# Half feed-forwards' up phases: two of the four weight sums of each tile pair made by accumulating loads from GpSimd instead of by VectorE

## The reference, cut to what matters

```python
def swiglu(h, wg, wu, wd):
    return (jax.nn.silu(h @ wg) * (h @ wu)) @ wd

def half_ffn(h, g, shift, scale, gate, wg, wu, wd):
    return h + 0.5 * gate * swiglu(modulate(rms_norm(h, g), shift, scale), wg, wu, wd)

for l in range(DEPTH):                      # DEPTH = 2, d = 1024
    x   = half_ffn(x,   ..., ffn_w_gate[l, 0], ffn_w_up[l, 0], ffn_w_down[l, 0])
    ctx = half_ffn(ctx, ..., the same weights)
    ...                                     # token mixing
    x   = half_ffn(x,   ..., ffn_w_gate[l, 1], ffn_w_up[l, 1], ffn_w_down[l, 1])
    if l < DEPTH - 1:
        ctx = half_ffn(ctx, ..., the same weights)
```

## Time and profile before

| | |
|---|---|
| median of three runs | 2948.27 us |
| span of the profiled execution, the only time the profile gives for it | 2949.2 us |
| PE busy | 2864.6 us, 97% |
| DVE busy | 1701.3 us, 58% |
| ACT busy | 602.0 us, 20% |
| POOL busy | 37.6 us, 1% |
| DMA, SP's queue, ACT's queue, the software queue | 31.6%, 7.6%, 0.9% of the 16 engines |

### The profile page before, as it was taken

How to read it: one execution, slowest core, us unless ns; L and a number is a source line. 1 busy time by engine, 2 the same in 40 slices (tenths; PEclk the granted TensorE clock), 3 DMA queues, 4 the chain that set the end, 5 groups by cost and what they waited for, 6 DMA issues and landing times.

```text
span 2949.2 us, 41107 instructions
## 1 busy us (share of the span) xinstructions
PE 2864.6 (97%) x16754; PEld 2354.5 (80%) x16754; DVE 1701.3 (58%) x3407; ACT 602.0 (20%) x1371; POOL 37.6 (1%) x60
## 2 busy tenths in 40 slices
PE   8988999999999999999999999999999999999999
PEld 7777788977889888888644468888888888766999
DVE  3376467345566477773225457775377773235775
ACT  1254221134221210000124420100021000134110
POOL 0000000020000000000000000000000000000000
PEclk9999999999999999999999999999999999999999
DMA  6400465663665534423213034442444433322454
GB/s 239 139 2 3 147 235 151 193 167 109 221 209 151 190 136 164 149 87 90 91 39 114 1 129 157 158 123 64 129 156 157 148 88 80 116 80 86 144 145 113
DMA packets 349215, 376.15 MB, mean 128 GB/s; under 512 B 7299, under 2 KB 302612, under 8 KB 348260
## 3 DMA queue, kind: packets, MB, share of 16 engines
q1 hardware_dynamic: 323748, 285.68, 31.6%
q10 hardware_dynamic: 23072, 82.52, 7.6%
q0 software_dynamic: 2208, 5.31, 0.9%
HBM read 372.44 MB, written 1.05 MB: 127 GB/s over the span
## 4 chain that ended last, share of the span: by engine, by line
PE 92%; DVE 4%; ACT 3%; issue 1%; DMA 0%; SPq 0%; DVEq 0%; ACTq 0%
PE acc L134 76%; PE aux L134 14%; ACT sb_xn L302 1%; PE aux L2563 1%; DVE sb_work L1570 1%; DVE sb_big L1400 0%; DMA sb_work<-c_decay 0%; DVE sb_work L1400 0%; PE aux L2020 0%; ACT sb_rstd L290 0%; DMA sb_x<-xT 0%; DVE sb_xn L278 0%; ACT sb_rstd L292 0%; DVE sb_work L2792 0%; ACT sb_big L1087 0%
## 5 line engine op out<-in xcount | busy, mean ns | idle before, releaser
L134 PE MATMUL acc<-sb_xn,weights 128*128 128x256 f32 (+3 forms) x5184 | 1221.8, 389 | 17.8 <-DVE sb_xn L278 8.2
L134 PEld LDWEIGHTS acc<-sb_xn,weights 128*128 128x128 f32 (+1 forms) x5184 | 943.2, 190 | 248.2 <-issue 124.3
L134 PE MATMUL acc<-sb_work 128*128 128x256 f32 (+1 forms) x1944 | 374.1, 346 | 2.9 <-DVE sb_work L1575 2.9
L134 PEld LDWEIGHTS acc<-sb_work 128*128 128x128 f32 x1944 | 323.6, 191 | 38.2 <-issue 4.0
L134 PE MATMUL acc<-sb_work,weights 128*128 128x256 f32 (+2 forms) x1508 | 322.0, 361 | 5.8 <-DVE sb_work L1617 3.6
L134 PE MATMUL acc<-sb_big,weights 128*128 128x256 f32 (+1 forms) x1776 | 315.0, 334 | 4.2 <-issue 4.0
L134 PEld LDWEIGHTS acc<-sb_big,weights 128*128 128x128 f32 x1776 | 279.0, 192 | 31.1 <-issue 5.5
L134 PEld LDWEIGHTS acc<-sb_work,weights 128*128 128x128 f32 x1508 | 254.1, 191 | 53.5 <-issue 25.6
L1537 ACT COPY sb_work<-acc 128x256 f32<-128x256 f32 (+1 forms) x108 | 36.7, 340 | 684.0 <-PE acc L134 684.0
L1610 DVE TENSOR_TENSOR sb_work<-sb_work,acc 128x256 f32<-128x256 f32 (+1 forms) x112 | 42.6, 380 | 218.0 <-PE acc L134 218.0
L1543 ACT ACTIVATE sb_work<-sb_work 128x256 f32<-128x256 f32 (+1 forms) x88 | 34.4, 391 | 562.3 <-DVE sb_work L1624 562.3
(11 more groups left out here) (352 smaller groups left out, 2671.4 us busy)
## 6 DMA issues: line engine op xcount, KB each, us to landing
weights<-ffn_w_up SPq DMA_DIRECT2D x88, 1024.0 KB, 9.1
weights<-ffn_w_down SPq DMA_DIRECT2D x48, 1408.0 KB, 7.2
sb_work<-w_mod_rows ACTq DMA_DIRECT2D x100, 512.0 KB, 6.2
weights<-ffn_w_gate SPq DMA_DIRECT2D x44, 1024.0 KB, 5.5
sb_big<-w_mod_rows ACTq DMA_DIRECT2D x44, 512.0 KB, 4.8
weights<-mix_w_in SPq DMA_DIRECT2D x5, 2048.0 KB, 11.7
weights<-ple_w_gate SPq DMA_DIRECT2D x4, 2048.0 KB, 7.9
weights<-na_w_qkv SPq DMA_DIRECT2D x8, 1024.0 KB, 8.0
```

What stands on the lines that cost most here:

```text
L134: return te.matmul(o, lhsT, rhs, start=start, stop=stop, skip_group_check=True)
```

## The change

In tiles 2 to 21 of the up phase of each half feed-forward (`by_dma`), s1 and s3 are no longer made by DVE. POOL makes them with loads, for a pair of tiles at a time (`gpsimd_fast`), with three DMAs of 128 partitions by 4 by 256 numbers (512 KB) each:

- a plain load of the upper k-tiles of the up weights into a buffer (`sum_pairs`, two of them, in turn);
- an accumulating load of the lower k-tiles of the gate weights onto those of the up weights in the weight slot, which makes s3 there;
- once the first has landed, an accumulating load of the lower k-tiles of the up weights onto the buffer, which makes s1 of both tiles.

A load can add but not subtract here, so s3 becomes a11 + a21, and the signs of the other sums, of the copy of product 1 (now an ACTIVATE with scale -1) and of one read of product 3 are changed to suit. For pair b, POOL starts when product 6 of tile 2b-3 is done (the last reader of that buffer); for the first pair, when the input of the half feed-forward is complete. DVE's s2 and PE's product 5 now wait for the pair's sum, PE's product 7 for the sum in the slot. The two buffers need room: the rows keep two tiles where they had three. s2 and s4 stay on DVE, as do all four sums of tiles 0 and 1 and of the down phases. Semaphores used earlier in the program are used again for the new waits, so `masks_or_pair_sum_arrived` and `rwkv_up_or_pair_sum_arrived` are the two buffers' and `rpb_or_slot_sum_arrived0` to `3` the four slots'.

```diff
+    sum_up = [area(work, 3072 + 512 * n, 4, 128) for n in range(2)]
+    sum_pairs = [area(work, 4096 + 1024 * n, 4, 256) for n in range(2)]
-    row_cond, row_tile = area(work, 8192, 2, D), [area(work, at, D) for at in (10240, 11264, 4608)]
+    row_cond, row_tile = area(work, 8192, 2, D), [area(work, at, D) for at in (10240, 11264)]
...
+        def by_dma(self, i):
+
+            return 2 <= i < FT
...
             for q in FIRST_PRODUCTS if i == 0 else PRODUCTS:
-                if q in SUM_FOR:
-                    te.wait_ge(st_s.sem, F.s(4 * j + (SUMS if i else FIRST_SUMS)[SUM_FOR[q]]))
+                if q == 5 and F.by_dma(i):
+                    te.wait_ge(pair_sum[i // 2 % 2].sem, F.pair[i // 2])
+                elif q == 7 and F.by_dma(i):
+                    te.wait_ge(slot_sum[F.up[i // 2].slot].sem, F.slot[i // 2])
+                elif q in SUM_FOR:
+                    te.wait_ge(st_s.sem, F.s(i, SUM_FOR[q]))
...
-                st_u.on(ac.copy(u[:, s, :], bank_a[:, 0:F.H]))
+                st_u.on(ac.activation(u[:, s, :], bank_a[:, 0:F.H], ACT.Copy, scale=-1.0))
...
+    def gpsimd_fast(F, w_gate, w_up, x_ready):
+        gv, uv = (w.rearrange("(k p) n -> p k n", p=128) for w in (w_gate, w_up))
+        gp.wait_ge(x_ready[0].sem, x_ready[1])
+        for b in range(1, FH):
+            c, blk = slice(256 * b, 256 * b + 256), F.up[b]
+            if b >= 2:
+                gp.wait_ge(F.done[2 * b - 3, 6][0].sem, F.done[2 * b - 3, 6][1])
+            pair_sum[b % 2].on(gp.dma_start(sum_pairs[b % 2], uv[:, 4:8, c]))
+            gp.wait_ge(weights_in[blk.slot].sem, blk.arrived_at)
+            up_low = slots[blk.slot][:, 2048:3072].rearrange("p (k n) -> p k n", k=4)
+            slot_sum[blk.slot].on(gp.dma_start(up_low, gv[:, 0:4, c], accum_op=ALU.add))
+            gp.wait_ge(pair_sum[b % 2].sem, F.pair[b] - 16)
+            pair_sum[b % 2].on(gp.dma_start(sum_pairs[b % 2], uv[:, 0:4, c], accum_op=ALU.add))
...
         for n in which:
-            if n == 0:
-                for blk in F.blocks_of(i):
+            if n in (0, 2) and F.by_dma(i):
+                continue
+            if n == 0 or n == 1 and F.by_dma(i):
+                for blk in F.blocks_of(i - i % 2 if i < FT else i):
                     ve.wait_ge(weights_in[blk.slot].sem, blk.arrived_at)
+            if n == 1 and F.by_dma(i):
+                ve.wait_ge(pair_sum[i // 2 % 2].sem, F.pair[i // 2])
...
-            st_c12.on(ve.tensor_tensor(g2, g2, bank_e[:, 0:F.H], ALU.add))
+            st_c12.on(ve.tensor_tensor(g2, bank_e[:, 0:F.H], g2, ALU.subtract))
...
-        for M in (mix0, mix1):
-            gpsimd_heads(M.heads)
+        for F, M in ((half00, mix0), (half01, None), (half10, mix1), (half11, None)):
+            w = [ins[name][F.l, F.j] for name in ("ffn_w_gate_2", "ffn_w_up_2")]
+            gpsimd_fast(F.fast, *w, F.norm.x_ready[KT - 1])
+            if M is not None:
+                gpsimd_heads(M.heads)
```

More of the change, by code:

```diff
@@ L138, in build @@
     hy_in, x_in = signal("hyena_tables_arrived", 16), signal("x_arrived", 16)
-    ctx_in, up_in = signal("dft_and_context_arrived", 16), signal("rwkv_up_arrived", 16)
-    msk_in, rpb_in = signal("masks_arrived", 16), [signal(f"rpb_arrived{q}", 16) for q in range(4)]
+    ctx_in, up_in = signal("dft_and_context_arrived", 16), signal("rwkv_up_or_pair_sum_arrived", 16)
+    msk_in, rpb_in = signal("masks_or_pair_sum_arrived", 16), [signal(f"rpb_or_slot_sum_arrived{q}", 16) for q in range(4)]
     p_in = signal("p_arrived", 16)
@@ L1349, in build @@
     FH = FT // 2
-    sum_up = [area(work, 3072 + 512 * n, 4, 128) for n in range(3)]
+    sum_up = [area(work, 3072 + 512 * n, 4, 128) for n in range(2)]
+    sum_pairs = [area(work, 4096 + 1024 * n, 4, 256) for n in range(2)]
+    pair_sum, slot_sum = [msk_in, up_in], rpb_in
+    for sig, loads in ((msk_in, 2), (up_in, 3), *zip(rpb_in, (9, 8, 8, 8))):
+        sig.reserve(loads)
     sum_down = [area(work, 8192 + FH * 128 * n, FH, 128) for n in range(3)]
@@ L1430, in __init__ @@
             m = n - self.start
-            self.s, self.t = st_s.reserve(4 * m), st_t.reserve(8 if up else 4)
+            made = [4 * min(i, 2) + 2 * max(0, min(i, FT) - 2) + 4 * max(0, i - FT) if up else 4 * (i - FT) for i in range(n)]
+            count = st_s.reserve((2 * 4 + 2 * (FT - 2) if up else 0) + 4 * KT // 2)
+            self.s = lambda i, k: count(made[i] + ({1: 0, 3: 1}[k] if self.by_dma(i) else (SUMS if i else FIRST_SUMS)[k]))
+            self.t = st_t.reserve(8 if up else 4)
+            self.pair = {b: pair_sum[b % 2].reserve(2)(1) for b in range(1, FH)} if up else {}
+            self.slot = {b: slot_sum[self.up[b].slot].reserve(1)(0) for b in range(1, FH)} if up else {}
             self.u, self.b, self.v, self.d, self.c12, self.c21 = (s.reserve(m) for s in (st_u, st_b, st_v, st_d, st_c12, st_c21))
@@ L1454, in activations, with sums @@
             return [src[:, kt * h:kt * h + kt, self.H * t:self.H * t + self.H] for h in range(2) for t in range(2)]
+        def sums(self, i):
+            c = 128 * (i % 2)
+            return [sum_pairs[i // 2 % 2][:, :, c:c + 128]] + sum_up if i < FT else sum_down
         def blocks_of(self, i):
@@ L1474, in tensor_fast @@
             a11, a12, s3, a22 = F.weights(i)
-            s1, s2, s4 = sum_up if up else sum_down
+            s1, s2, s4 = F.sums(i)
             t1, t2, t4 = F.sum_x if up else F.sum_h
@@ L1522, in scalar_first_copy @@
         ac.wait_ge(F.done[0, 1][0].sem, F.done[0, 1][1])
-        st_u.on(ac.copy(F.temps[0][:, 0, :], bank_a[:, 0:F.H]))
+        st_u.on(ac.activation(F.temps[0][:, 0, :], bank_a[:, 0:F.H], ACT.Copy, scale=-1.0))
     def scalar_fast(F, following=None):
@@ L1553, in scalar_fast @@
             scalar_square(following, KT - 1)
+    def gpsimd_fast(F, w_gate, w_up, x_ready):
[11 more added lines that the diff above has]
+            pair_sum[b % 2].on(gp.dma_start(sum_pairs[b % 2], uv[:, 0:4, c], accum_op=ALU.add))
     def vector_weight_sums(F, i, which):
         a11, a12, a21, a22 = F.weights(i)
-        s1, s2, s4 = sum_up if i < FT else sum_down
+        s1, s2, s4 = F.sums(i)
         for n in which:
-            if n == 0:
-                for blk in F.blocks_of(i):
+            if n in (0, 2) and F.by_dma(i):
+                continue
+            if n == 0 or n == 1 and F.by_dma(i):
+                for blk in F.blocks_of(i - i % 2 if i < FT else i):
                     ve.wait_ge(weights_in[blk.slot].sem, blk.arrived_at)
+            if n == 1 and F.by_dma(i):
+                ve.wait_ge(pair_sum[i // 2 % 2].sem, F.pair[i // 2])
             if i not in (F.start, FT) and n != 2:
@@ L1565, in vector_weight_sums @@
                 ve.wait_ge(F.done[i - 1, q][0].sem, F.done[i - 1, q][1])
-            if n:
-                ve.wait_ge(st_s.sem, F.s(4 * (i - F.start) + (SUMS if i else FIRST_SUMS)[n] - 1))
-            to, one, other, op = ((s1, a21, a22, ALU.add), (s2, s1, a11, ALU.subtract),
-                                  (a21, a11, a21, ALU.subtract), (s4, a12, s2, ALU.subtract))[n]
-            st_s.on(ve.tensor_tensor(to, one, other, op))
+            if n and not (n == 1 and F.by_dma(i)):
+                ve.wait_ge(st_s.sem, F.s(i, {1: 0, 2: 1, 3: 1 if F.by_dma(i) or not i else 2}[n] if i or n != 2 else 3))
+            to, one, other = ((s1, a21, a22), (s2, s1, a11), (a21, a11, a21), (s4, a12, s2))[n]
+            st_s.on(ve.tensor_tensor(to, one, other, ALU.add))
     def vector_activation_sums(F, i):
@@ L1579, in vector_activation_sums @@
             vector_weight_sums(F, 0, (2,))
-        st_t.on(ve.tensor_tensor(b12, b22, b12, ALU.subtract))
+        st_t.on(ve.tensor_tensor(b12, b12, b22, ALU.subtract))
         ve.wait_ge(st_t.sem, st_t.n)
```

## The result

The changed kernel is slower by 0.8%: 2972.06 us in the median of four runs (2967.63 to 2976.64) against 2948.22 for the kernel before, a ratio of 1.008 [1.0067, 1.0092], which is 20 to 27 us. The profiled execution has a span of 2972.0 us, 22.8 more than that of before (2949.2). From here on a ratio in brackets is a 95% interval against the kernel before, and "up phase of `half11`" is the stretch from PE's wait at its start (2742.74 before) to its last wait (2876.30 before), 133.56 us.

A forecast was written before the change was run, and what follows sets the result against it. PE was taken to bound the kernel. The span 2949.2 + 10 (late loads in `half11`) - 0.5 (removed sums) = 2958.7 us, less 0.9 to the median 2957.8, stated as 2957; range 2947 to 3035.

The forecast's parts named there:

- What bounds the kernel: Whole kernel: PE makes 92% of the chain of waits, DVE 4%, so the removed work is hardly on the path.
- Removed, -0.5 us: DVE's 160 sums, 109 us, go; only waits at phase ends can shrink: 0.5 us, all in `half11`, bounds 0 and 6.2.
- Signs and ACT's copy, 0: DVE's adds keep their shape and ACT's copy becomes a same-shape ACTIVATE, covered by two products: zero.
- Wide phases, the sums hidden, 0: Wide phases: the last load lands at 19.4 us, due at about 28 after POOL may start, so zero cost.
- `half11`, +10 us: Up phase of `half11`: the third load lands late, holding DVE's s2 and then PE's product 4: 10 us over nine pairs.
- Every second pair is late: In `half11` a 2.3 us wait delays the next burst, so the next pair makes it: 1.15 us on the mean.
- hidden everywhere: Rival: the software queue gets turns beside SP's burst, so all loads are in time: 2948 us, chance 0.34.
- The price of the accumulation: DMA engines: an accumulating load takes k = 2.5 times a plain load's 1.42 us, so 3.55 us.
- The rows, 0: Two row buffers: a row is issued behind product 1 of its tile, DVE waits up to 1.7 us, hidden: zero.
- The cover of 5.2 us: Behind DVE's row wait stands the read of product 4, which PE needs three products, 5.2 us, later.
- The rival of late rows: Two row buffers: POOL's 1.5 MB a pair delay rows beyond the cover, so PE waits: 2954 to 2970 us, chance 0.05.
- what would show it: Signs: for, `half11` 5 to 25 us longer with product 4 waits; against, PE waits in wide phases or at product 7.

The follow-up runs named there:

- e9: The changed kernel with four pair buffers instead of two in `half11`, so POOL may start a pair's loads two pairs earlier: 2956.12 us, ratio 1.0024.
- e7: The changed kernel with no accumulating load and three row buffers, leaving the signs, ACT's scaled copy and product 3's turned read: 2947.49 us, ratio 0.9997.
- e5: The changed kernel with both passes of a row always in one tile: 2962.74 us, ratio 1.0047.
- e12: The changed kernel with accumulating loads only in the wide phases and both passes of a row in one tile: 2947.98 us, ratio 0.9996.
- e3: The changed kernel with accumulating loads only in `half11`, three row buffers and DVE's sums in the wide phases: 2961.2 us, ratio 1.0048.
- e4: The changed kernel with both accumulating loads as plain loads of the same size, so the sums are wrong: 2956.75 us, ratio 1.0035.
- e1: The kernel before with only the row buffers changed, two instead of three: 2967.63 us, ratio 1.007.
- e11: The kernel before with two row buffers and both passes of a row always in one tile: 2946.94 us, ratio 1.0.
- e10: The changed kernel with only the accumulation onto the weight slot made a plain load, so s3 is wrong: 2965.68 us, ratio 1.0055.
- e8: The kernel before with the rows ended at tile 18 instead of 20 and s4 of tile 22 made later: 2940.41 us, ratio 0.9972.
- e2: The changed kernel with accumulating loads only in the three wide phases, DVE making the sums in `half11`: 2958.04 us, ratio 1.003.

## Why the prediction was right, and where it was not

*What bounds the kernel: right.* PE is dense, of the removed 109 us of DVE less than 1 us came back as time, and whatever comes late in front of product 4 is paid in full and with a restart.

*Removed, -0.5 us: right.* In `half11` the 0.40 went and the 0.99 stayed (e9's 132.99 us against 133.56). The 0.35 us at the end of `half10` weren't foreseen.

*Signs and ACT's copy, 0: right* (e7).

*Wide phases, the sums hidden, 0: right* (e5, e12).

*`half11`, +10 us: the place and the chain right, 13.0 to 14.2 measured; that the size is so near is in part luck.* The wait is at product 4, released by the read of product 7, behind s2's wait for the third load, L1591 beyond 10 us, as forecast. The waits alone are 8.9 us (8.7 in e3, 9.9 in e5) for the forecast's 10. What the sum put at nothing is the restart, 0.54 us for each of seven waits, 3.8 in all, and the clock, 1.4.

The waits come out near 10 though their pattern is another one. "Every second pair is late" by 2.3 us is what the prediction has; in the changed kernel seven of nine pairs wait (eight in e3), 1.3 us each on the mean, and the first of them, the pair that the prediction works out, 1.67. The 2.3 us that a wait gives to the next pair were taken as pure gain; but SP's block hangs on the same product 4 and comes as much later, and the third load, which goes out 5 to 6 us after POOL's start, lands behind that block and not ahead of it. After the first wait SP's block is issued 5.2 us after POOL's start, where the working has 3.6. Waits of 1.67 and 0.55 follow each other, so some of the relief is there. The error of the same kind on the queue: POOL's data don't stand still beside a burst, only a load that begins in it does. The rival "hidden everywhere" rested on just the half of this that is true.

The price of the accumulation was taken as 2.5 x 1.42 = 3.55 us. As a ratio it is 2.0, half of a plain load's rate, as the Trainium skill has it ("Collectives: The Full Stack", The bandwidth ceiling: the fold count and why AG ≠ RS ≠ AR). In us it is 3.46 by the share, almost the forecast's figure, since the plain load is dearer here as well, and 2.7 on engines that are free (e4). Put into the prediction's working, these two land at 16.2 and 14.7, 2.1 and 0.6 us late. So the runs don't show this term to be wrong, only to be loose. (In the earlier trace rows the slices of the block run from 303 to 394 GB/s, not from 315 to 397; nothing hangs on it.)

*The rows, 0: wrong*, by 7.7 us. The step that failed is "a row is issued only behind product 1 of the tile that uses it": in ten tiles it is issued in the tile after. The landing forecast (up to 9.6 us, some more beside POOL's loads) was fair: the rows landed in 3.3 to 11.1 us. The cover of 5.2 us is near the 5.5 measured, but by luck: it was worked out for the read of product 4, and what the late pass holds up is the read of product 7 of the next tile. The error was in the order of the program: the count of passes at each tile, with the odd ones, would have shown it. The rival of late rows (0.05) had the price, 2954 to 2970, and the place, but put the cause at POOL's traffic; e1 has the waits without that traffic.

*The sum:* 2949.2 + 10 - 0.5 against 2949.2 + 13.5 + 7.7 and 1.6 more in stages that have no new wait. The forecast of 2957 is 15 us low; half of it is the rows, and 4.0 are what `half11` takes over its term. That the time lies in the stated range is luck in so far as the range was left wide for dearer accumulations (k up to about 4.3), not for late rows or restarts.

*Wrong in "what would show it":* PE's waits in the wide phases, named there as a sign against the forecast, came, from another cause than the one considered. The slot's sum was always in time, as expected: PE has no new wait at product 7.

## What to carry to other kernels

When a buffer is taken from a rotation, write down for each step which load is issued where and which use comes first, odd steps included; one line that kept a row's two passes in one tile was worth 20 us here (e1, e11). A chain of dependent loads is timed from its start to the use, and its lateness went with an earlier start and the same bytes (a deeper rotation, e9), and with both additions left out (e4), while one of them left out took away only a third (e10); shares of the DMA engines that add up to over 100% don't prove that they are full. And work taken from an engine that doesn't bound the kernel gave nothing even where it was moved for free (e12), while the same profile's few waits at the ends of the phases were worth 6 us in the trace and 8 in the medians without moving any (e8).

## What was not expected of the hardware

- A load that accumulates goes in 528 packets where a plain one of the same shape has 144, and takes the engines 3.46 us against 1.70 by the share (2.7 us alone on them). POOL itself takes 1.3 us to issue it, against 0.78.
- Two queues that are both under way share packet by packet (229 to 235), but a software-queue load issued together with a hardware-queue block of 2 MB moves 1 packet in 2 us of it and 79 in the next 2. The third load of a pair so lands 10.6 us after its issue in the median, where the second, which accumulates as well, takes 7.3.
- A wait of PE can cost more than itself through the clock. After 2.52 us of idling in `half11` of the changed kernel the granted clock fell:

```profile
2815.00:2819.00 4.00, 3.28 (x16) 3.28 (x17) 2.56 (x9) 0.48 (x2) 1.27 (x1) 0.61 0.88 136
2819.00:2823.00 4.00, 4.00 (x36) 4.00 (x36) 1.35 (x5) 0.28 (x1) 0.00 (x0) 0.96 1.08 197
```

  The product there took 1.93 us, where it takes 1.16 behind the other waits, and the tile 1.4 us more. The length of the wait doesn't decide it: the clock fell after 2.99 and 3.73 us in e1 and after 2.16 us in e4 (0.77 from 1112 to 1116), and not after 2.90 us in e1, 2.23 in e2, or 2.17 and 2.19 in the changed kernel. In e1 this was 4.6 of 17 us.
